# A decoder layer on one core: four rooms for value pages, three for key pages, transposes dealt out between matmuls, and an MLP in token halves

## The chip, the core and the metric

The kernel runs on one core of a Trainium2 chip. A core has a matrix engine (TensorE, PE in the rows; its weight loads are PEld), a vector engine (VectorE, DVE), an activation engine (ScalarE, ACT), a general engine (GpSimd, POOL) and SyncE (SP), which here only issues transfers. Each works through its own list of instructions in order; engines wait for each other on semaphores. Matmuls write to PSUM, eight banks of 128 partitions by 512 fp32 numbers. The metric is the device time of one execution in microseconds (us); lower is better.

## The reference, cut to what matters

One decoder layer is applied to 512 prompt tokens and to 64 sample tokens (8 sequences of 8 tokens, each with 512 cached positions in four pages of 128):

```python
h = rms_norm(x, ln1_pre) * (1 + sc1) + sh1            # shifts, scales, gates from c @ ada_w
u, q, k, v, qi, ki, wi = split(h @ w_in)
mixed = concat(pool_mix(u), sparse_attention(q, qi, wi, k, v, ki))   # top 128 or 130 keys a query
x = x + g1 * rms_norm(mixed @ w_out, ln1_post)
h = rms_norm(x, ln2_pre) * (1 + sc2) + sh2
f = square(relu(h @ w_ff1)) @ w_ff2                   # 1024 -> 4096 -> 1024
x = x + g2 * rms_norm(f, ln2_post)
```

The samples' keys and values come partly from the paged caches `cache_k` and `cache_v`, through `page_table`. All is fp32.

## The kernel before

Every large product is split for accuracy: an operand is stored as a high part (`fp32r`, rounded by ScalarE) and a low part (the rest, by VectorE), and hi·hi + hi·lo + lo·hi are summed in PSUM. A weight of 1 MB (a "piece": 1024 rows by 256 columns, or 512 by 512) comes by DMA into `raw`, is split into `w_split` by ScalarE (`hi_until`) and VectorE (`lo_until`), and is then used. Both buffers have two rooms.

The program is written out by hand, one list of instructions for each engine; their order is the order of the code. Its stages:

1. **Head.** The first eight `ada` pieces give shift and scale as rows (`modulation`), which are turned into columns in `mod_t` (`turned_modulation`). The normalised tokens are transposed in eight chunks of 128 features (`turned_hidden`); ScalarE scales and shifts each chunk into `stage`, rounds it into `act_hi`, VectorE makes `act_lo`. The first projection (`qi`) goes through the eight chunks in order (`first_pair`).
2. **Projections, indexer, top-k, prompt attention.** `lg` are the logits of one of 32 (query block, head) pairs, `pv` their values. In between, the other 16 `ada` pieces are used.
3. **Cached attention of the samples.** For each sequence b, SyncE loads four key pages and four value pages (256 KB each; `load_pages`), TensorE turns the keys (`turn_pages`, banks `KT`), then for each pair of sequences bp comes `sample_logits`, the softmax on VectorE and ScalarE, `turn_sample_probs`, `sample_values` and `turn_sample_output`. Keys have two rooms in `pages`, values two in `v_pages`; b uses room b % 2. Values are loaded from the last prompt `pv` on; a room's next keys after its last `KT` bank, its next values after `pvR` of the pair.
4. **Output projection** (`wo`), residual, second norm; `turned_hidden(1)` transposes the eight chunks and then the samples' rows.
5. **MLP**, in four quarters of `w1` (16 pieces in all) and `w2`. For a piece of `w1`, `project` makes two chunks of 128 hidden features for the 512 prompt tokens (moving operand `act_hi`, `act_lo`, 128x512), then the 64 samples by rows: the samples' hi and lo parts (`act_s`, 128 columns) are the weights and the piece's hi and lo the moving operand (`rows_s`, eight matmuls of 512 columns). The two halves of that result are added and turned by `fold_pending` (plain fp32, through `halves_mlp`). ScalarE takes relu, VectorE squares, and both split again into `hid_hi`, `hid_lo`, `hid_s` for `w2` (`by_token`).

All matmuls are issued in the helper `mm` (line 747), all transposes in `turn` (line 750), nearly all ScalarE work in `run` (line 1294), so names of tiles tell more than lines.

## Time and profile before

| | |
|---|---|
| Median of 3 runs | 910.16 us (906.89 to 914.69) |
| The profiled execution | 910.76 us, its span 909.1 us |
| TensorE busy | 832.8 us, 92% of the span |
| VectorE, ScalarE, GpSimd busy | 443.4, 329.2, 88.9 us |
| Mean granted TensorE clock | 0.957 of full speed |
| Bytes moved | 105.85 MB, 116 GB/s on average |

The span runs from the first to the last instruction; 1.7 us of the device time lie outside it. A matmul's shown length includes a drain that overlaps the next one, so rates are read from the starts. In rows, `128*128 128x512` is a weight of 128 by 128 and a moving operand of 512 columns. An fp32 matmul stands twice in the trace, an fp32r matmul once.

### The profile page before, as it was taken

The numbers are of one execution on the slowest core, as the hardware profiler recorded it, in microseconds if no ns is written. First come the engines' busy times: TensorE is split into PE (matmuls) and PEld (weight loads), VectorE is DVE, ScalarE is ACT, GpSimd is POOL, SyncE is SP. The second block draws the span as 40 slices with busy tenths as digits, with TensorE's granted clock in tenths as the row PEclk, the third lists the DMA queues.
The fourth block names the chain that finished last, engine by engine and source line by source line (L and its number), as shares of the span: only waits on it lengthen the run. The fifth ranks groups of instructions, "written<-read, shape, count | busy, mean of one in ns | idle before, by whom it ended". The sixth has DMA issues, their size and how long they took to land.

```text
span 909.1 us, 11559 instructions
## 1 busy us (share of the span) xinstructions
PE 832.8 (92%) x4338; PEld 638.3 (70%) x4338; DVE 443.4 (49%) x819; ACT 329.2 (36%) x611; POOL 88.9 (10%) x144
## 2 busy tenths in 40 slices
PE   2799999799988987789969999999999999999997
PEld 0377557587745566547847888888888888888875
DVE  0351666999767864412655422243333343244255
ACT  2462542133355653403463422343213241134332
POOL 2141301011623320010010000000000000000000
PEclk9989999798989998969979999999999999999999
DMA  9833311022367677682112123222212222321202
GB/s 318 293 101 104 102 47 45 16 91 92 96 226 267 212 250 252 218 313 67 47 47 93 49 91 93 70 69 93 90 54 89 93 72 67 93 93 50 90 0 105
DMA packets 68779, 105.85 MB, mean 116 GB/s; under 512 B 6986, under 2 KB 32214, under 8 KB 68714
## 3 DMA queue, kind: packets, MB, share of 16 engines
q1 hardware_dynamic: 64194, 96.48, 32.3%
q0 software_dynamic: 3296, 6.39, 2.3%
q10 hardware_dynamic: 1232, 2.23, 0.7%
q8 instruction: 35, 0.57, 0.3%
q14 instruction: 22, 0.18, 0.1%
HBM read 100.04 MB, written 5.15 MB: 116 GB/s over the span
## 4 chain that ended last, share of the span: by engine, by line
PE 80%; DVE 6%; DMA 6%; ACT 3%; issue 2%; SPq 2%; DVEq 0%; POOL 0%; ACTq 0%
PE bank L747 77%; PE bank L750 3%; DMA pages<-in_ada_w 2%; DMA pages<-in_cache_k 2%; SPq L562 2%; DVE score L1817 1%; DMA raw<-in_ada_w 1%; DVE small L1813 1%; ACT w_split L1269 1%; ACT stage L1294 1%; DMA v_pages<-in_cache_v 1%; DVE w_split L496 1%; DVE x_res L1998 0%; DMA out_v_p<-stage 0%; DVE x_nrm L1714 0%
## 5 line engine op out<-in xcount | busy, mean ns | idle before, releaser
L747 PE MATMUL bank<-act_hi,w_split 128*128 128x512 f32 (+1 forms) x800 | 265.5, 401 | 5.5 <-DVE q_lo L1698 5.5
L747 PEld LDWEIGHTS bank<-act_hi,w_split 128*128 128x128 f32 (+1 forms) x800 | 152.0, 190 | 42.6 <-issue 7.4
L496 DVE TENSOR_TENSOR w_split<-raw,w_split 128x2048 fp32r<-128x2048 f32 (+2 forms) x47 | 105.5, 2247 | 127.0 <-ACT w_split L1269 126.9
L747 PE MATMUL bank<-w_split,hid_hi 128*128 128x512 f32 x512 | 159.0, 392 | 0.0
L747 PE MATMUL bank<-act_lo,w_split 128*128 128x512 f32 (+1 forms) x400 | 157.9, 395 | 0.0
L1269 ACT ACTIVATE w_split<-raw 128x2048 fp32r<-128x2048 f32 (+2 forms) x48 | 89.3, 1862 | 96.1 <-PE bank L747 96.0
L747 PEld LDWEIGHTS bank<-w_split,hid_hi 128*128 128x128 f32 x512 | 95.9, 188 | 20.9
L747 PE MATMUL bank<-w_split,hid_lo 128*128 128x512 f32 x256 | 100.3, 392 | 0.0
L747 PEld LDWEIGHTS bank<-act_lo,w_split 128*128 128x128 f32 (+1 forms) x400 | 76.3, 191 | 15.1
L1294 ACT ACTIVATE stage<-bank 128x512 f32<-128x512 f32 (+3 forms) x51 | 30.0, 589 | 98.3 <-PE bank L747 91.3
L747 PE MATMUL bank<-w_split,act_s 128*128 128x512 f32 (+1 forms) x248 | 60.7, 387 | 1.5 <-DVE out_t L2004 1.5
L747 PE MATMUL bank<-w_split,act_hi 128*128 128x512 f32 x192 | 61.2, 400 | 0.0
L747 PEld LDWEIGHTS bank<-w_split,hid_lo 128*128 128x128 f32 x256 | 48.1, 188 | 10.4
L2048 DVE TENSOR_TENSOR stage<-stage 128x512 f32<-128x512 f32 x32 | 22.2, 692 | 67.3 <-ACT stage L1294 65.8
L747 PEld LDWEIGHTS bank<-w_split,act_s 128*128 128x128 f32 x248 | 46.0, 188 | 11.3 <-issue 1.9
L747 PEld LDWEIGHTS bank<-w_split,act_hi 128*128 128x128 f32 x192 | 36.6, 193 | 8.3 <-issue 0.8
L747 PE MATMUL bank<-w_split,act_lo 128*128 128x512 f32 x96 | 38.1, 397 | 0.0
L747 PE MATMUL bank<-w_split,hid_s 128*128 128x512 f32 x128 | 32.0, 392 | 2.2 <-DVE out_t L2076 2.2
L1294 ACT ACTIVATE probs<-probs,small 128x128 f32<-128x128 f32 (+4 forms) x36 | 20.9, 580 | 31.7 <-DVE small L1893 20.5
L747 PE MATMUL bank<-raw,c_pad 128*32 128x512 f32 x160 | 27.4, 764 | 5.3 <-DMA raw<-in_ada_w 5.2
L1294 ACT ACTIVATE stage_s<-bank 128x128 f32<-128x128 f32 (+1 forms) x24 | 9.2, 384 | 62.5 <-PE bank L747 62.5
L1294 ACT ACTIVATE half_s<-bank 64x512 f32<-64x512 f32 x10 | 5.9, 595 | 65.5 <-PE bank L747 65.5
(247 smaller groups left out, 1061.2 us busy)
## 6 DMA issues: line engine op xcount, KB each, us to landing
raw<-in_w_ff SPq DMA_DIRECT2D x32, 1024.0 KB, 5.4
raw<-in_ada_w SPq DMA_DIRECT2D x20, 1024.0 KB, 5.3
raw<-in_w_in SPq DMA_DIRECT2D x10, 1024.0 KB, 5.5
pages<-in_cache_k SPq DMA_DIRECT2D x32, 256.0 KB, 5.3
v_pages<-in_cache_v SPq DMA_DIRECT2D x32, 256.0 KB, 4.2
pages<-in_ada_w SPq DMA_DIRECT2D x4, 1024.0 KB, 12.5
raw<-in_w_out SPq DMA_DIRECT2D x4, 1024.0 KB, 6.9
x_in<-in_x_prompt SPq DMA_DIRECT2D x1, 2048.0 KB, 14.6
```

The source lines that it names most:

```text
L496: return ops.tensor_tensor(lo, r, hi.bitcast(F32), ALU.subtract)
L562: sp.dma_start(slots[:, b % 2, g, :], cache[bass.ds(page[b * NPG + g], 1)].rearrange("o p n -> (o p) n"))\
L747: return nc.tensor.matmul(out, lhsT, rhs, start=start, stop=stop, skip_group_check=True)
L750: return nc.tensor.transpose(out, in_, cc("ident")[0:k, 0:k])
L1269: return nc.scalar.activation(hi, r, ACT.Copy)
L1294: return nc.scalar.activation(out, in_, func, **kw)
L1813: link(nc.vector.max(top8[0:r, :], buf))
L1817: link(nc.vector.match_replace(buf, top8[0:r, :], buf, TAKEN))
L2048: nc.vector.tensor_tensor(stage[:, n % 2, :], stage[:, n % 2, :], stage[:, n % 2, :], ALU.mult)\
```

## The change

- **Cached attention.** `v_pages` gets four rooms and `k_more` is a third room for keys. Both lie where the prompt's `q_hi` to `k_lo` and `qiv_hi` were. The values of sequences 0 to 3 are loaded once the last two `lg` banks are full; the third key room after the last `pv`. The two first `wo` pieces are loaded after these values and after the keys of sequence 4, where they came before all of them.
- **Head.** `turned_modulation(0)` is cut into quarters between the `ada` pieces; four of the eight chunks and the samples' rows are transposed between the steps of the first `qi` matmuls. On ScalarE the split of the first `qi` piece stands ahead of the last `ada` rows, on VectorE ahead of `mod_t`.
- **MLP.** The tokens are two halves of 256 prompt and 32 sample tokens (HN = 288), in `tok_hi` and `tok_lo`. A unit is 128 hidden features for one half: 24 matmuls with 288 moving columns. A piece has four units, in three banks that rotate. `rows_s`, the fold and `halves_mlp` are gone from the MLP. The samples' rows are transposed first; three chunks follow, and the other five stand between the steps of the first three units.

```diff
@@ plan_banks @@
-            take(("w1", 8 * f + 2 * i), 0), take(("w1", 8 * f + 2 * i + 1), 1)
-            take(("w1R", 4 * f + i), 2), take(("w1S", 4 * f + i), 2)
+            for u in range(4):
+                take(("w1", 8 * f + 2 * i + u // 2, u % 2), (4 * i + u) % 3)
@@ SyncE @@
-            for n in range(AT[("ada", 12)] + 2, AT[("wo", 0)] + 2):
+            for n in range(AT[("ada", 12)] + 2, AT[("wo", 0)]):
                 load_piece(n)
+            full(sp, ("lg", N_AT - 2))
+            full(sp, ("lg", N_AT - 1))
+            for b in range(4):
+                load_pages(b, cv, v_rooms, v_page_in)
+            load_piece(AT[("wo", 0)])
             full(sp, ("pv", N_AT // 2 - 1))
...
+            load_pages(2, ck, k_rooms, k_page_in)
+            for b in (3, 4):
+                full(sp, ("KT", b - 3, 3))
+                load_pages(b, ck, k_rooms, k_page_in)
+            load_piece(AT[("wo", 1)])
+            for b in (5, 6):
+                full(sp, ("KT", b - 3, 3))
+                load_pages(b, ck, k_rooms, k_page_in)
+            full(sp, ("pvR", 0))
+            for b in (4, 5):
+                load_pages(b, cv, v_rooms, v_page_in)
...
@@ TensorE, head @@
+            for i in range(4):
                 modulation(i)
+            out = claim(("modT", 0))
+            turned_quarter(out, 0)
+            modulation(4)
+            turned_quarter(out, 1)
+            modulation(5)
...
+                    if kc < 4:
+                        turned_chunk(0, x_nrm, kc + 4)
+                    elif kc == 4:
+                        turned_rows(0, x_nrm)
@@ TensorE, MLP @@
+            def unit_step(out, hi, lo, j, x, kc):
+                cols = slice(128 * j, 128 * j + 128)
+                mm(out[:, 0:HN], hi[:, kc, cols], tok_hi[:, kc, x, :], kc == 0, False)
+                mm(out[:, 0:HN], hi[:, kc, cols], tok_lo[:, kc, x, :], False, False)
+                return mm(out[:, 0:HN], lo[:, kc, cols], tok_hi[:, kc, x, :], False, kc == KC - 1)
...
+                    for kc in range(KC):
+                        pe.wait_ge(S["h_hi"], KC + kc + 1)
+                        pe.wait_ge(S["h_low"], KC + kc + 1)
+                        for out, (j, x) in zip(outs, units):
+                            last = unit_step(out, hi, lo, j, x, kc)
...
+                        if kc + 3 < KC:
+                            turned_chunk(1, out_t, kc + 3)
@@ VectorE @@
+            lo_until(AT[("qi", 0)] + 1)
             turned_hidden(0)
-            lo_until(AT[("qi", 0)] + 1)
...
+                else:
+                    stage_rows(1)
                 if j:
                     normalise(2, LATE[j - 1], out_t, x_res)
```

SyncE's list between the last `ada` pieces and the first keys of the cached attention, before; a name in brackets is a semaphore that the row waits for (`bank_full7`: the last `pv`; `bank_full0` to `bank_full2`: a `KT` bank).

```order
L535 DMA raw<-in_w_out 128x4x512 [waits ada_half]
L535 DMA raw<-in_w_out 128x4x512 [waits bank_full0]
L562 DMA v_pages<-in_cache_v 128x512 [waits bank_full7]
L562 DMA v_pages<-in_cache_v 128x512 x7
L562 ISA [waits bank_full0]
L562 DMA pages<-in_cache_k 128x512
```

The same place after; `bank_full4,bank_full3` are the last two `lg`.

```order
L576 DMA v_pages<-in_cache_v 128x512 [waits bank_full4,bank_full3]
L576 DMA v_pages<-in_cache_v 128x512 x7
...
L548 DMA raw<-in_w_out 128x4x512 [waits ada_half]
L576 DMA k_more<-in_cache_k 128x512 [waits bank_full7]
L576 DMA k_more<-in_cache_k 128x512 x3
L576 DMA pages<-in_cache_k 128x512 [waits bank_full0]
L576 DMA pages<-in_cache_k 128x512 x3
L576 ISA [waits bank_full1]
L576 DMA pages<-in_cache_k 128x512
```

The value pages now stand ahead of the first `wo` piece and wait for logits instead of values; keys of sequence 2 wait for the last `pv` alone.

TensorE in the MLP before, at the end of a piece of `w1`, the start of the next one, and its fold.

```order
L747 MATMUL bank1<-act_lo,w_split 128x512
L747 MATMUL bank1<-act_hi,w_split 128x512
L747 MATMUL bank2<-w_split,act_s 128x512 [waits bank_free2]
L747 MATMUL bank2<-w_split,act_s 128x512 x7
L747 MATMUL bank0<-act_hi,w_split 128x512 [waits bank_free0,lo_ready]
L747 MATMUL bank0<-act_lo,w_split 128x512
...
L747 MATMUL bank0<-act_hi,w_split 128x512
L747 MATMUL bank2<-cst,halves_mlp 128x64 [waits bank_free2]
L747 MATMUL bank2<-cst,halves_mlp 128x64 x3
L747 MATMUL bank1<-act_hi,w_split 128x512 [waits bank_free1]
```

The same place after, from the end of one unit into the next.

```order
L770 MATMUL bank2<-tok_lo,w_split 128x288
L770 MATMUL bank2<-tok_hi,w_split 128x288
L770 MATMUL bank0<-tok_hi,w_split 128x288 [waits bank_free0]
L770 MATMUL bank0<-tok_lo,w_split 128x288
L770 MATMUL bank0<-tok_hi,w_split 128x288 x2
L770 MATMUL bank0<-tok_lo,w_split 128x288
```

The sample rows and the folds are gone, and every matmul is 288 columns wide.

TensorE in the head before (`c_pad` rows are `ada` pieces, `mod_rows` the turn of the modulation, `x_nrm` chunks of tokens).

```order
L747 MATMUL bank<-raw,c_pad 32x512 x8
L750 MATMUL bank<-cst,rows_in 128x52
L750 MATMUL bank<-cst,x_nrm 128x128 x16
L747 MATMUL bank<-pages,c_pad 32x512 x8
L747 MATMUL bank<-cst,mod_rows 128x9 x16
L750 MATMUL bank<-cst,x_nrm 128x128 x16
L750 MATMUL bank<-cst,x_nrm 128x64 x8
L747 MATMUL bank<-act_hi,w_split 128x512
L747 MATMUL bank<-act_lo,w_split 128x512
```

The same place after.

```order
L770 MATMUL bank<-cst,mod_rows 128x9 x4
L770 MATMUL bank<-raw,c_pad 32x512 x4
L770 MATMUL bank<-cst,mod_rows 128x9 x4
L770 MATMUL bank<-raw,c_pad 32x512 x4
L773 MATMUL bank<-cst,rows_in 128x52
L770 MATMUL bank<-pages,c_pad 32x512 x4
L770 MATMUL bank<-cst,mod_rows 128x9 x4
L770 MATMUL bank<-pages,c_pad 32x512 x4
L773 MATMUL bank<-cst,x_nrm 128x128 x8
L770 MATMUL bank<-cst,mod_rows 128x9 x4
L773 MATMUL bank<-cst,x_nrm 128x128 x8
L770 MATMUL bank<-act_hi,w_split 128x512
```

Three of the four quarters of the modulation's turn now stand between `ada` pieces, and the matmuls with `act_hi` begin after four chunks instead of eight and the samples' rows.

## Rows read from the trace of the kernel before

**Rows 1.** The page, part 4: shares by engine of the chain that ended last.
```profile
PE 80%; DVE 6%; DMA 6%; ACT 3%; issue 2%; SPq 2%; DVEq 0%; POOL 0%; ACTq 0%
```

**Rows 2.** Busy time by stretch: us, PE, PEld, DVE, ACT, POOL, PEclk, DMA, GB/s.
```profile
473.00:600.00 127.00, 127.00 (x564) 102.60 (x563) 46.69 (x50) 43.95 (x59) 0.00 (x0) 1.00 0.24 75
```

**Rows 3.** Instructions in order of time, TensorE, MLP: start, us, operation, count.
```profile
501.23 1.98 PE L747 MATMUL bank<-w_split,act_s 128*128 128x512 f32 x8
...
508.48 1.00 PE L747 MATMUL bank<-cst,halves_mlp 128*128 128x64 f32 x8
...
522.09 1.00 PE L747 MATMUL bank<-cst,halves_mlp 128*128 128x64 f32 x8
```

**Rows 4.** The same view, two earlier stretches with narrower moving operands.
```profile
90.24 1.15 PE L747 MATMUL bank<-w_split,act_s 128*128 128x272 f32 x8
...
329.11 0.28 PE L747 MATMUL bank<-keys,qiv_hi 128*128 128x256 f32 x1
...
329.58 0.28 PE L747 MATMUL bank<-turned_hi,qiv_lo 128*128 128x256 f32 x1
```

**Rows 5.** One tile (act_s, MLP): weight loads' durations min/median/max ns.
```profile
L747 PEld LDWEIGHTS bank<-w_split,act_s x128: 187/188/188, 483.3 to 847.5; 128*128 128x128 f32 x128
```

**Rows 6.** Order of time, TensorE, cached attention; brackets: idle before, releaser.
```profile
321.79 0.40 PE L747 MATMUL bank<-k_hi,q_lo 64*128 64x512 f32 x2
...
345.12 6.08 PE L750 MATMUL bank<-cst,pages 128*128 128x128 f32 x32 [4.03 <-DMA pages<-in_cache_k]
351.04 0.60 PE L750 MATMUL bank<-cst,probs 128*128 128x128 f32 x4
...
357.42 3.94 PE L750 MATMUL bank<-cst,pages 128*128 128x128 f32 x32
...
373.41 3.25 PE L750 MATMUL bank<-cst,pages 128*128 128x128 f32 x16 [2.19 <-DMA pages<-in_cache_k]
...
390.47 1.94 PE L747 MATMUL bank<-v_pages,p_t 128*32 128x128 f32 x32 [2.01 <-DMA v_pages<-in_cache_v]
...
397.29 2.96 PE L747 MATMUL bank<-mod_rows,cst 128*128 128x512 f32 x3
```

**Rows 7.** The same view of SyncE's DMA issues.
```profile
333.47 3.68 SPq L562 DMA_DIRECT2D v_pages<-in_cache_v  x8
```

**Rows 8.** The same view of VectorE, cached attention.
```profile
354.84 0.56 DVE L1937 CUSTOM_DVE_ANT_0 probs<-bank,small 128x384 f32<-128x384 f32 x1 [2.91 <-PE bank L747]
...
357.69 0.23 DVE L1952 TENSOR_TENSOR p_new<-probs,cst 128x64 f32<-128x64 f32 x1
...
379.55 4.49 DVE L496 TENSOR_TENSOR w_split<-raw,w_split 128x2048 fp32r<-128x2048 f32 x2 [1.41 <-ACT w_split L1269]
```

**Rows 9.** The same view of ScalarE there.
```profile
377.61 3.72 ACT L1269 ACTIVATE w_split<-raw 128x2048 fp32r<-128x2048 f32 x2
```

**Rows 10.** The same view of all engines, before the first projection.
```profile
38.74 1.90 ACT L1269 ACTIVATE w_split<-raw 128x2048 fp32r<-128x2048 f32 x1
...
43.36 2.29 DVE L496 TENSOR_TENSOR w_split<-raw,w_split 128x2048 fp32r<-128x2048 f32 x1
43.36 0.78 ACT L1294 ACTIVATE stage<-bank,mod_t 128x512 f32<-128x512 f32 x1 [2.72 <-DVE mod_t L1729]
...
50.60 0.79 PE L747 MATMUL bank<-act_hi,w_split 128*128 128x512 f32 x1
```

**Rows 11.** The same view, into the MLP.
```profile
462.88 0.17 DVE L1709 RECIPROCAL rstd<-rstd 128x1 f32<-128x1 f32 x1 [0.68 <-ACT rstd L1294]
...
472.46 0.50 PE L747 MATMUL bank<-act_hi,w_split 128*128 128x512 f32 x1
```

**Rows 12.** Busy time by stretch, columns as in rows 2.
```profile
36.00:42.80 6.80, 5.92 (x51) 4.15 (x49) 0.13 (x1) 2.40 (x2) 1.68 (x3) 1.00 0.71 223
42.80:53.00 10.20, 7.80 (x30) 5.70 (x31) 6.68 (x9) 9.20 (x14) 4.54 (x9) 0.50 0.41 83
...
341.10:345.10 4.00, 0.00 (x0) 0.00 (x0) 1.12 (x6) 0.00 (x0) 0.00 (x0) 0.76 1.05 393
```

More of the change, by code:

```diff
@@ L51 @@
 UW = 16 + TP + DB * SEG
+HP, HS = TP // 2, TS // 2
+HN = HP + HS
 def t5_bucket(n):
@@ L285, in build_program @@
         w_split = sb("w_split", [128, NSPLIT, 4096], F32R)
-        act_hi = sb("act_hi", [128, KC, TP], F32R)
-        act_lo = sb("act_lo", [128, KC, TP], F32R)
+        first = ExitStack()
+        act_hi = sb("act_hi", [128, KC, TP], F32R, first)
+        q_s = sb("q_s", [128, 4, TS], stack=first)
+        k_s = sb("k_s", [128, 4, TS], stack=first)
+        act_lo = sb("act_lo", [128, KC, TP], F32R, first)
+        ki_s = sb("ki_s", [128, TS], stack=first)
+        wi_t = sb("wi_t", [8, TS], stack=first)
+        ident_r = sb("ident_r", [128, 128], F32R, first)
+        first.close()
+        tok_hi = sb("tok_hi", [128, KC, 2, HN], F32R)
+        tok_lo = sb("tok_lo", [128, KC, 2, HN], F32R)
         act_s = sb("act_s", [128, KC, 2 * TS], F32R)
@@ L402, in build_program @@
         stage_out = [sem("stage_out0"), sem("stage_out1")]
-        k_page_in = [sem("k_page_in0"), sem("k_page_in1")]
-        v_page_in = [sem("v_page_in0"), sem("v_page_in1")]
+        k_page_in = [sem(f"k_page_in{i}") for i in range(3)]
+        v_page_in = [sem(f"v_page_in{i}") for i in range(4)]
+        k_rooms = [pages[:, 0, :, :], pages[:, 1, :, :], k_more[:, :, :]]
+        v_rooms = [v_pages[:, i, :, :] for i in range(4)]
         block = ctx.enter_context(nc.Block())
@@ L585, in _ @@
+            full(sp, ("pvR", 0))
+            for b in (4, 5):
+                load_pages(b, cv, v_rooms, v_page_in)
+            full(sp, ("KT", 4, 3))
+            load_pages(7, ck, k_rooms, k_page_in)
+            full(sp, ("pvR", 1))
+            for b in (6, 7):
+                load_pages(b, cv, v_rooms, v_page_in)
             for n in range(AT[("wo", 0)] + 2, len(PIECES)):
@@ L801, in _, with turned_quarter, turned_rows @@
-            for i in range(6):
-                modulation(i)
+            def turned_quarter(out, g):
+                evacuated(pe, ("ada", 2 * g + 1))
+                for j in range(4 * g, 4 * g + 4):
+                    last = mm(out[:, 9 * j:9 * j + 9], mod_rows[:, 128 * j:128 * j + 128], cc("sel_t"), True, True)
+                return last
+            def turned_rows(k, src):
+                out = claim(("hTS", k))
+                for kc in range(KC):
+                    last = turn(out[:, TS * kc:TS * kc + TS], src[0:TS, NT, 128 * kc:128 * kc + 128], TS)
+                done(last, ("hTS", k))
@@ L803, in _, with turned_chunk @@
+            def turned_chunk(k, src, kc):
+                out = claim(("hT", k, kc))
+                for t in range(NT):
+                    last = turn(out[:, 128 * t:128 * t + 128], src[:, t, 128 * kc:128 * kc + 128], 128)
+                done(last, ("hT", k, kc))
+            for i in range(4):
+                modulation(i)
+            out = claim(("modT", 0))
[3 more added lines that the diff above has]
+            modulation(5)
             pe.wait_ge(S["small_in"], 96)
@@ L804, in _ @@
             done(turn(claim("rowsT")[:, 0:52], rows_in[:, :], 52), "rowsT")
-            turned_hidden(0, x_nrm, range(4), False)
-            for i in range(6, 8):
-                modulation(i)
-            turned_modulation(0)
-            turned_hidden(0, x_nrm, range(4, KC))
+            modulation(6)
+            turned_quarter(out, 2)
+            modulation(7)
+            pe.wait_ge(S["normed"], NT + 1)
+            for kc in range(2):
+                turned_chunk(0, x_nrm, kc)
+            done(turned_quarter(out, 3), ("modT", 0))
@@ L811, in _ @@
+            for kc in range(2, 4):
+                turned_chunk(0, x_nrm, kc)
             hidden_ready = []
@@ L1160, in turn_pages @@
                     for g in range(NPG):
-                        last = turn(out[:, 128 * g:128 * g + 128], pages[:, b % 2, g, 128 * c:128 * c + 128], 128)
+                        last = turn(out[:, 128 * g:128 * g + 128], k_rooms[b % 3][:, g, 128 * c:128 * c + 128], 128)
                     done(last, ("KT", b, c))
@@ L1328, in turned_hidden @@
                 act.wait_ge(S["mod_ok"], 2 * (k + 1))
+                if k:
+                    act.wait_ge(S["hs_staged"], 2)
+                    run(tok_hi[:, :, :, HP:HN], stage_s[:, :, :].rearrange("p c (x t) -> p c x t", x=2)).then_inc(S["hs_hi"], 1)
                 for kc in range(KC):
```

179 lines of the change are left out of this document (93 added, 86 removed).

## The prediction

> **What bounds the kernel now.** I read the chain that ended last first: four fifths of it are TensorE [rows 1], so a wait elsewhere counts only where TensorE stands still for it. Then busy time by stretch. In the MLP TensorE has no gap at all: 127.0 of 127.0 us, at a granted clock of 1.00 [rows 2]. There only fewer matmul columns help. The gaps are in three other places, and the instructions in order of time show what ends them: the cached attention waits for pages [rows 6], the head for the first projection's operands [rows 10], the MLP for its first chunk [rows 11]. The change touches these four places, so the sum has four terms. It is made against the profiled execution, 910.8 us (span 909.1 and 1.7 outside it), which lies 0.6 above the median of 910.16.
>
> **The MLP's units.** Before, a piece takes from one fold to the next 522.09 - 508.48 = 13.61 us [rows 3]. It holds 48 chunk matmuls and 8 sample matmuls of 512 columns, and the fold. Between the start of the sample matmuls at 501.23 and the fold at 508.48 lie 32 matmuls of 512 columns [rows 3]: 7.25 / 32 = 0.2266 us each. After, a piece is 4 units x 24 = 96 matmuls of 288 columns. No row has 288, but two are near. Five matmuls of 256 columns start within 0.47 us, 0.1175 each; eight of 272 take 1.15 us, less the 0.28 that one lasts, so 0.124 each [rows 4]. The line through 256 and 512 rises by 0.000426 us a column and gives 0.1175 + 32 x 0.000426 = 0.131 for 288. A piece is then 96 x 0.131 = 12.6 us, 1.02 less, and 16 pieces save **16.3 us**. Bounds: if 288 cost as much a column as 256 do, 0.1322, the saving is 14.7; if as little as 512 do, 0.1275, it is 21.9. I take the line, since the 272 row lies within 0.001 of it. Of the 1.02, the fold gives 0.92 (13.61 - 56 x 0.2266) and 1,024 columns fewer give 0.44; 40 more matmuls, each with a fixed 0.0084 on that line, take 0.34 back.
>
> The Trainium skill, "TensorE: Matmul & The Clock Gate", section "Back-to-back issue gap", puts a warm matmul at its columns over 2.4 GHz and 2.5 ns. That is 122.5 ns for 288 columns, an estimate by which a piece takes 11.8 us and the whole comes to about 866. The rows disagree: for 512 columns the rule says 216 ns and they show 227, so the measurement decides.
>
> Nothing else in a piece should reach TensorE. A unit lasts 3.1 us and a bank comes back two units (6.3 us) later. ScalarE needs two relus and two roundings for a pair of units, VectorE a square and two subtractions, and both are busy for about a third of this stretch [rows 2]. The weight split at a piece's end delays a relu by about 2 us, less than the 6.3. If that cover failed, each piece would lose the excess, up to 2 us.
>
> **Into the MLP.** Before, the last norm's reciprocal is at 462.88 after an idle wait of 0.68, and the first matmul at 472.46, since all transposes come first [rows 11]. After, VectorE puts two sample operations ahead of that reciprocal, about 0.75 each, of which the idle time takes 0.7: norm 0.8 later, first transpose about 464.8. A chunk needs four transposes (32 take 3.94 us at full clock [rows 6], so 0.5, or 1.0 at half), scaling (0.78, as in the head [rows 10]), rounding and subtraction (about as long): first matmul at about 468.2, 4.3 earlier. But five chunks, 5 x 0.5 = 2.5 us, now stand between matmuls, where they were hidden by the wait. Net 1.8; but the granted clock can fall to half around such a start, as in the head (0.50 from 42.8 to 53.0 [rows 12]), and then falls on matmuls instead of transposes, at up to 3 us. So between -1 and +2; I take **1.0 saved**.
>
> **Head.** Before, VectorE splits the first weights (2.29 us) after `mod_t`, ahead of the first `act_lo`, and TensorE begins the projection only at 50.60, after all transposes [rows 10]. After, ScalarE's split (1.90 us) waits for the weights, which land at about 38: the DMA queues are busy for 0.71 of 36.0 to 42.8 [rows 12], so until about 40.8, and one more megabyte behind them takes near 3 us. Then come the last modulation rows, a quarter of the turn (the full one has 32 records) and `mod_t`, with VectorE's split just ahead of it at about 42. The first scaling stays near 43, where it was (43.36), but the low part no longer queues behind 2.29 us, and TensorE can start at about 45, 5.6 earlier. It pays for four chunks and the sample rows between matmuls, 2.6 us at full clock, 5 at half, and at the clock of 0.50 [rows 12] much of this may run at half. Between 0 and 4; I take **1.5 saved**.
>
> **Cached attention.** TensorE waits 4.03 us for keys of sequence 2, 2.19 for a later pair, 2.01 for values [rows 6], 8.2 us in these three alone, and the work behind each is slow: 32 transposes take 6.08 us after the first wait and 3.94 us without one [rows 6]. After, values wait for the last `lg`, whose matmuls end at 322.2, instead of 333.47 [rows 6, 7]: 11 us sooner. From there I follow TensorE. Logits of pair 0 end at 341.1, where the 4.03 begins. Two sequences of keys take 4.0; probabilities, logits and values of one pair take 357.42 - 351.04 = 6.4 [rows 6]; VectorE's softmax takes from 354.84 to 357.92, 3.1 [rows 8], hidden after the first pair. So keys 2 and 3 end at 345.3, the first softmax lets go at about the same time, pair 0 ends at 352.0, keys 4 and 5 at 356.0, pair 1 at 362.8 with its output, keys 6 and 7 at 367, pair 2's output with the logits of pair 3 near 371.
>
> Here the next limit stands: ScalarE's split of the two `wo` pieces (3.72 us) and VectorE's (4.49, it waits for them) come right after pair 1's output, ahead of the last softmax [rows 8, 9]. They start near 368.3 instead of 377.6, VectorE's ends near 375, softmax at 378, then transposes, values and output of the last pair, 5.5 to 7.5 us with their handovers and a possible half clock. The gates come at 383.5 to 386 instead of 397.29 [rows 6]. Saved 11.3 to 13.8, I take **12.5**. Bounds: 6, if key pages 2 still come as late as before (below), and 15, if the `wo` splits don't bind.
>
> Edits with one answer: the first key rooms and the `ada` loads don't move; GpSimd's list is unchanged; the output projection and the second MLP product keep their matmuls.
>
> **Sum.** 16.3 + 1.0 + 1.5 + 12.5 = 31.3; 910.8 - 31.3 = **879.5 us**.
>
> **Rivals.**
> 1. *The pages stay late.* SyncE's list now holds 16 value pages and a `wo` piece, 5.2 MB, ahead of the third key room. With the four key pages that is 6.3 MB from 322.6 on. At the 393 GB/s of 341.1 to 345.1 [rows 12] the keys land near 339; under 286 GB/s they land at 345, where they came before. For it speaks that one queue carries all; against it that the queue stands still before 333 for want of a room. It costs the 4.03 and about 2 of slow work behind it: 885.5.
> 2. *Slower: the weight load sets the pace.* Each matmul loads its own weights, and a load lasts 188 ns [rows 5]. 512 columns cover that at 227; 288 columns at 131 don't, if a load can't begin before the one ahead has finished. Then a piece takes 96 x 0.188 = 18.0 us, 4.4 more than before, 16 pieces 71 more, and with the other terms 910.8 - 15.0 + 71 = 967. It decides from 0.142 us a matmul (13.61 / 96) for the MLP by itself, and from 0.152 ((16 x 13.61 + 15) / 1536) for the whole. Against it: the 272-column rows have the same loads and come every 0.124 us. The same page of the Trainium skill, section "Step-by-step: what each phase is for", lets a load run under the matmul before it; these rows agree.
> 3. *The small matmuls cost no more a column than the large ones.* Then the units save 21.9, not 16.3: 874.
> 4. *Both new starts give nothing*, because the half clock falls on matmuls and the transposes between them cost what the earlier start gives: 882.
>
> **How the numbers follow.** Chances: forecast, 874.5 to 884, 0.62; rival 1, 0.14; rival 3, 0.10; rival 4 falls into the forecast's range; rival 2, 0.04; several misses on the gain's side with a result still under 901, 0.06; a new stall that leaves less than 9 us, 0.04. The range of 868 to 891 takes in rivals 1, 3 and 4 and one further term at its lower bound (879.5 + 6.5 + 2.5 = 888.5, and 3 for scatter among runs); below it and above it I leave about 0.15. A measurement here tells about 1% from no change, which is 901 to 919. Faster by more: 0.93; within: 0.03; slower: 0.04.
>
> **What would show it.** Units every 3.1 to 3.2 us in the MLP with TensorE still full and `tok_hi` matmuls 0.131 apart; VectorE and ScalarE never the releaser of a unit's bank. In the cached attention no idle time that a page ends; value pages issued right after the last `lg`; the gates near 385 less what the head gives; the last wait there ended by VectorE's softmax behind the `wo` split. First matmuls 5 to 6 us earlier in the head and 4 in the MLP, each followed by transposes between matmuls. The prediction is wrong if the distance of unit matmuls is above 0.135, if the third key room lands after TensorE asks for it, or if one of the starts moves later.

## The result

The changed kernel takes 887.38 us (median of 4 executions, 884.9 to 889.27) where the kernel before took 912.42 beside it: a ratio of 0.9728, 95% interval 0.9667 to 0.979. In a second series, described below, it was 0.9714 (0.9677 to 0.9751). The forecast was 879.5 with a range of 868 to 891, so it held the sign and the range; the gain is about 25 us, where 31.3 were forecast.

The page of the changed kernel, parts 1, 4 and 5 (in the last: busy us, mean ns, and idle time before with what ended it):

```profile
PE 815.1 (92%) x4850; PEld 657.7 (74%) x4850; DVE 441.2 (50%) x819; ACT 325.5 (37%) x627; POOL 89.0 (10%) x144
...
PE 81%; DVE 7%; DMA 5%; ACT 3%; issue 2%; SPq 1%; DVEq 0%; POOL 0%; ACTq 0%
...
L770 PE MATMUL bank<-tok_hi,w_split 128*128 128x288 f32 x1024 | 207.8, 297 | 0.6 <-DVE tok_lo L1774 0.6
```

TensorE has 512 matmuls more than before and is busy for 17.7 us less. The chain is bounded as before [rows 1]. The units' matmuls waited 0.6 us in all, once, for the first chunk.

Busy time by stretch (us; PE, PEld, DVE, ACT, POOL; granted clock; DMA share; GB/s): the stretch of rows 2, then the second quarter's `w1` and its `w2`:

```profile
473.00:600.00 127.00, 127.00 (x775) 114.64 (x774) 45.65 (x52) 42.26 (x68) 0.00 (x0) 1.00 0.26 83
566.48:617.36 50.88, 50.88 (x385) 50.88 (x384) 20.98 (x26) 19.06 (x34) 0.00 (x0) 1.00 0.25 83
617.36:668.65 51.29, 51.29 (x227) 42.07 (x225) 17.47 (x17) 9.23 (x8) 0.00 (x0) 1.00 0.26 82
```

TensorE is still full at full clock [rows 2]. Four pieces are 384 matmuls in 50.88 us, so 0.1325 us each and 12.72 us a piece, where it was 13.61 [rows 3].

TensorE in order of time, cached attention (start, us; in brackets the idle time before and what ended it):

```profile
343.31 2.00 PE L773 MATMUL bank<-cst,k_more 128*128 128x128 f32 x16 [1.71 <-DMA k_more<-in_cache_k]
345.95 2.00 PE L773 MATMUL bank<-cst,pages 128*128 128x128 f32 x16 [0.64 <-DMA pages<-in_cache_k]
...
374.79 1.08 PE L770 MATMUL bank<-v_pages,p_t 128*32 128x128 f32 x32 [0.66 <-ACT p_t L1369]
...
378.98 0.44 PE L773 MATMUL bank<-cst,pv_rows 128*128 128x128 f32 x2 [1.40 <-ACT pv_rows L1369]
...
386.47 4.08 PE L770 MATMUL bank<-mod_rows,cst 128*128 128x512 f32 x8
```

The three long waits for pages [rows 6] are down to 1.71 and 0.64, both at the start; the gates begin at 386.47, where it was 397.29. What SyncE, ScalarE and VectorE do there, in the same view:

```profile
322.86 9.11 SPq L576 DMA_DIRECT2D v_pages<-in_cache_v  x16
...
333.98 1.95 SPq L576 DMA_DIRECT2D k_more<-in_cache_k  x4
```

```profile
370.10 3.72 ACT L1344 ACTIVATE w_split<-raw 128x2048 fp32r<-128x2048 f32 x2
```

```profile
372.04 4.49 DVE L509 TENSOR_TENSOR w_split<-raw,w_split 128x2048 fp32r<-128x2048 f32 x2 [1.41 <-ACT w_split L1344]
```

Values are issued 10.6 us earlier than before [rows 7]; the splits of the `wo` pieces stand where they stood [rows 8, 9], 7.5 us earlier.

The head of the changed kernel, all engines, same view:

```profile
40.30 2.29 DVE L509 TENSOR_TENSOR w_split<-raw,w_split 128x2048 fp32r<-128x2048 f32 x1 [9.17 <-ACT w_split L1344]
...
43.20 0.78 ACT L1369 ACTIVATE stage<-bank,mod_t 128x512 f32<-128x512 f32 x1 [2.44 <-DVE mod_t L1808]
...
45.57 0.47 PE L770 MATMUL bank<-act_hi,w_split 128*128 128x512 f32 x1 [2.78 <-DVE act_lo L1774]
...
59.16 2.29 DVE L509 TENSOR_TENSOR w_split<-raw,w_split 128x2048 fp32r<-128x2048 f32 x1 [1.04 <-ACT w_split L1344]
...
62.20 0.47 PE L770 MATMUL bank<-act_hi,w_split 128*128 128x512 f32 x1 [0.92 <-DVE qiv_lo L1774]
```

The first matmul is at 45.57 instead of 50.60 [rows 10], after a split that VectorE now does ahead of `mod_t`. At 62.20 TensorE waits again: VectorE's split of the second `qi` piece stands behind the samples' rows and ahead of `qiv_lo`. TensorE, into the MLP:

```profile
451.88 2.82 PE L773 MATMUL bank<-cst,out_t 128*128 128x128 f32 x12 [7.92 <-DVE out_t L1793]
455.34 0.58 PE L770 MATMUL bank<-tok_hi,w_split 128*128 128x288 f32 x1 [0.64 <-DVE tok_lo L1774]
...
455.96 0.68 PE L770 MATMUL bank<-tok_hi,w_split 128*128 128x288 f32 x2
...
456.44 0.44 PE L770 MATMUL bank<-tok_lo,w_split 128*128 128x288 f32 x1
```

The first matmul of the MLP is at 455.34 instead of 472.46 [rows 11]. But the two starting at 455.96 and the next at 456.44 are 0.24 apart, nearly twice the distance of the later ones. Busy time by stretch shows why: the granted clock is 0.50 there, until 460.4.

```profile
446.70:460.40 13.70, 7.88 (x34) 7.49 (x35) 7.85 (x12) 7.49 (x12) 0.87 (x1) 0.50 0.24 77
```

**Where the time went, by stages.** From the starts in order of time of each kernel, experiments included, I took six lengths. "Head" is the start of the eight 272-column matmuls [rows 4]; "prompt" goes from the first to the last group of `lg` matmuls; "cached" from the last `pv` matmul to the first of `wo`; "into MLP" from the last `act_hi` matmul of `wo` (0.23 us before its last one) to the first of `w2`, four pieces included; then the second quarter's `w1` and `w2`. All in us.

| profile of | head | prompt | cached | into MLP | w1 | w2 |
|---|---|---|---|---|---|---|
| before | 90.24 | 64.97 | 70.01 | 74.87 | 53.52 | 52.39 |
| changed | 87.98 | 67.77 | 56.83 | 72.49 | 50.88 | 51.29 |
| changed, second profile | 89.28 | 64.18 | 60.51 | 72.33 | 50.88 | 51.29 |
| cached part alone | 94.28 | 64.10 | 61.02 | 76.48 | 53.52 | 52.39 |
| head alone | 89.64 | 64.51 | 70.12 | 74.87 | 53.54 | 52.39 |
| MLP alone | 91.19 | 68.12 | 66.50 | 72.63 | 50.88 | 51.29 |
| late values | 90.89 | 67.54 | 64.15 | 72.43 | 50.88 | 51.29 |
| spread `wo` splits | 90.87 | 64.10 | 57.27 | 72.44 | 50.88 | 51.29 |
| early key room | 91.09 | 64.20 | 56.93 | 72.58 | 50.88 | 51.29 |
| both of these | 89.87 | 65.07 | 53.51 | 72.24 | 50.88 | 51.29 |
| turns first | 89.88 | 65.10 | 59.41 | 72.01 | 50.88 | 51.29 |
| 256 columns | 90.02 | 67.29 | 55.39 | 67.11 | 45.81 | 51.28 |
| quarter fold | 92.11 | 70.51 | 66.32 | 72.87 | 51.53 | 51.72 |

The second quarter of the MLP repeats to 0.02 us wherever the code is the same. The other stages do not: the prompt attention, whose code no kernel here changes, takes 64.1 to 70.5 us.

Nor does the last `w2`, which none of the six lengths holds. TensorE, after the same wait there, in the first and then in the second profile of the changed kernel:

```profile
849.71 3.54 PE L770 MATMUL bank<-w_split,hid_s 128*128 128x512 f32 x8 [2.21 <-DVE out_t L2168]
```

```profile
851.82 2.07 PE L770 MATMUL bank<-w_split,hid_s 128*128 128x512 f32 x8 [2.21 <-DVE out_t L2168]
```

In the first the granted clock is 0.50 from 849.5 to 852.9, in the second it stays at 1.00. From the first matmul of the last `w2` to the end the two take 61.45 and 59.95 us. The clock falls in this place in six of the thirteen profiles: the first of the changed kernel, cached part alone, head alone, MLP alone, early key room and turns first.

### The profile page after: what moved, and what is told of

The parts are those of the page before. It is cut to its first block, busy times and chain, and to the rows that moved or that the text cites. A ratio compares the mean times of both kernels' runs of the same rounds, so it can differ in the third digit from the quotient of the medians.

```text
span 883.1 us, 12590 instructions
## 1 busy us (share of the span) xinstructions
PE 815.1 (92%) x4850; PEld 657.7 (74%) x4850; DVE 441.2 (50%) x819; ACT 325.5 (37%) x627; POOL 89.0 (10%) x144
## 4 chain that ended last, share of the span: by engine, by line
PE 81%; DVE 7%; DMA 5%; ACT 3%; issue 2%; SPq 1%; DVEq 0%; POOL 0%; ACTq 0%
PE bank L770 78%; PE bank L773 3%; DMA pages<-in_ada_w 2%; ACT w_split L1344 1%; DVE score L1908 1%; DVE small L1904 1%; DMA pages<-in_cache_k 1%; DMA raw<-in_w_in 1%; DVE w_split L509 1%; DMA raw<-in_ada_w 1%; ACT stage L1369 1%; DMA out_v_p<-stage 1%; DVE x_res L2089 0%; DVE keys L1774 0%; DVE probs L1984 0%
## 5 line engine op out<-in xcount | busy, mean ns | idle before, releaser
L770 PE MATMUL bank<-tok_hi,w_split 128*128 128x288 f32 x1024 | 207.8, 297 | 0.6 <-DVE tok_lo L1774 0.6
L770 PEld LDWEIGHTS bank<-tok_hi,w_split 128*128 128x128 f32 x1024 | 165.9, 189 | 2.2 <-issue 2.0
L770 PE MATMUL bank<-tok_lo,w_split 128*128 128x288 f32 x512 | 151.6, 296 | 0.0
L770 PE MATMUL bank<-act_hi,w_split 128*128 128x512 f32 (+1 forms) x288 | 102.4, 416 | 9.2 <-DVE q_lo L1777 5.5
L770 PEld LDWEIGHTS bank<-tok_lo,w_split 128*128 128x128 f32 x512 | 96.9, 189 | 0.1
L1369 ACT ACTIVATE stage<-bank 128x288 f32<-128x288 f32 (+3 forms) x83 | 36.9, 447 | 121.6 <-PE bank L770 114.5
L770 PEld LDWEIGHTS bank<-act_hi,w_split 128*128 128x128 f32 (+1 forms) x288 | 55.2, 192 | 26.0 <-issue 9.6
L2143 DVE TENSOR_TENSOR stage<-stage 128x576 f32<-128x576 f32 x32 | 24.3, 759 | 76.0 <-ACT stage L1369 76.0
L770 PE MATMUL bank<-act_lo,w_split 128*128 128x512 f32 (+1 forms) x144 | 57.8, 401 | 0.0
L770 PEld LDWEIGHTS bank<-act_lo,w_split 128*128 128x128 f32 (+1 forms) x144 | 27.9, 194 | 5.2
```

Source lines behind the costliest of these rows:

```text
L770: return nc.tensor.matmul(out, lhsT, rhs, start=start, stop=stop, skip_group_check=True)
L1369: return nc.scalar.activation(out, in_, func, **kw)
L2143: nc.vector.tensor_tensor(st, st, st, ALU.mult).then_inc(S["w1_squared"], 1)
```

## The experiments

**One part at a time.** Three kernels, each the kernel before with one part of the change.

Cached part alone, its core:

```diff
-                        load_pages(b, cv, v_pages, v_page_in)
...
+            full(sp, ("lg", N_AT - 2))
+            full(sp, ("lg", N_AT - 1))
+            for b in range(4):
+                load_pages(b, cv, v_rooms, v_page_in)
...
+            load_pages(2, ck, k_rooms, k_page_in)
```

> The kernel before with only the part on the pages changed: four rooms for value pages and a third for key pages, loaded as in the changed kernel; head and MLP as before. Theory A (the ledger by stages: the gains are those of three parts that do not touch each other): 13.2 us less than the kernel before, nearly all of it between the last prompt matmul and the first out projection, so about 899 us where the kernel before takes 912.4; the first gate matmul some 10 to 11 us earlier than in the kernel before, the head and every MLP piece as before. Theory B (pages are ready earlier only because the head starts the prompt attention 2.3 us earlier, or the MLP's later work gives part of it back): less than 10 us.

Measured: 905.82 us beside 913.2 (ratio 0.9923, 0.9896 to 0.9951), 7.4 less. So neither theory as put: below 10, but for another reason than B names, since this kernel's head was no earlier. Its first wait is the one of the changed kernel, and longer; TensorE, same view:

```profile
348.17 3.27 PE L771 MATMUL bank<-cst,k_more 128*128 128x128 f32 x16 [2.60 <-DMA k_more<-in_cache_k]
...
392.97 5.76 PE L768 MATMUL bank<-mod_rows,cst 128*128 128x512 f32 x8
```

Transposes that take 2.00 us in the changed kernel take 3.27 here, and gates that take 4.08 take 5.76.

Head alone, its core:

```diff
-            turned_hidden(0, x_nrm, range(4), False)
...
+            turned_quarter(out, 0)
+            modulation(4)
...
+                    if k == 0 and kc < 4:
+                        turned_chunk(0, x_nrm, kc + 4)
```

> The kernel before with only the head changed: turns between the modulation's matmuls, and the splits of the first query piece ahead of the last modulation. Theory A (ledger): 2.3 us less until the first matmul of the prompt's scores, and the prompt attention as long as before (64.97 us from its first to its last score matmul), so 910 us where the kernel before takes 912.4. Theory B (the 2.8 us that the prompt attention lost in the changed kernel follow from the shift of the head, which moves where the clock falls): prompt attention 67 to 68 us here too, and the whole within 0.7 us of the kernel before.

Measured: 909.5 us beside 913.2 (0.9954, 0.9933 to 0.9974), 3.7 less, with a prompt attention of 64.51. Theory B falls: the head's shift does not lengthen the prompt attention.

MLP alone, its core:

```diff
-                    project("w1", 4 * f + i)
+                    hidden_units(4 * f + i)
```

> The kernel before with only the MLP changed: units of 256 prompt and 32 sample columns, no fold, and its own turns between matmuls. Theory A (ledger): 13.5 us from the pieces and 0.3 us at the start the other way, so 13.2 us less, about 899 us; a piece of 96 matmuls lasts 12.7 us where it lasted 13.6. Theory B (the pieces are only quicker because the cached attention hands over earlier and loads of weights run further ahead): a piece of 13.2 us or more, and under 8 us less in all.

Measured: 899.78 us beside 913.2 (0.9855, 0.9807 to 0.9902), 13.4 less, pieces as in the changed kernel. Theory A holds. The three parts give 7.4 + 3.7 + 13.4 = 24.5, the whole about 25 to 26: the parts add up.

**The same kernel again.** No edit.

> The changed kernel itself once more, for the spread of its stages between two profiled executions of the same code. Theory A (the stages' differences in one pair of profiles carry chance of where the clock falls): its prompt attention, first to last score matmul, lies anywhere between 64 and 68 us (67.78 in its first profile), its head up to 3 us later than in its first profile (87.98 us at the end of the key index projection), its stretch from the last prompt matmul to the first out projection 55 to 61 us, and its MLP quarters, where the clock does not fall, are the same to 0.1 us. Theory B (the stages are set by the code): every stage within 0.3 us of the first profile. The median by both some 887 us.

Measured: 886.9 us beside 913.08 (0.9714, 0.9677 to 0.9751). Theory A holds at every stage. Busy time by stretch of its prompt attention, after that of the first profile:

```profile
254.53:322.30 67.77, 59.48 (x388) 35.23 (x388) 50.68 (x179) 39.41 (x120) 23.14 (x37) 0.85 0.71 235
```

```profile
256.68:320.86 64.18, 56.80 (x389) 33.27 (x388) 50.36 (x177) 39.36 (x120) 23.18 (x37) 0.89 0.74 249
```

The same instructions, with VectorE and ScalarE busy for as long to 0.4 us; the granted clock is 0.85 in one and 0.89 in the other. And its gates, with the stretch around them:

```profile
386.97 5.83 PE L770 MATMUL bank<-mod_rows,cst 128*128 128x512 f32 x8
```

```profile
380.30:390.50 10.20, 9.14 (x87) 4.27 (x86) 0.45 (x2) 1.41 (x5) 1.88 (x3) 0.50 0.15 53
```

The clock is 0.50 until 390.5, into the gates, which then take 5.83 us. In the first profile it was back at full before they began, and they took 4.08. So in these two profiles a stage with waits has a length that is good only to 2 to 4 us.

**The splits off the last wait.** The changed kernel with the `wo` splits in earlier gaps:

```diff
@@ ScalarE, after p_t of pair bp @@
+                if bp < 2:
+                    hi_until(AT[("wo", 0)] + 1 + bp)
...
-                if bp == 1:
-                    hi_until(AT[("wo", 0)] + 2)
@@ VectorE, before the peaks of pair bp + 1 @@
+                if bp in (1, 2):
+                    lo_until(AT[("wo", 0)] + bp)
...
-                if bp == 1:
-                    lo_until(AT[("wo", 0)] + 2)
```

> The changed kernel with the splits of the two first out-projection pieces moved off the wait for the last softmax: ScalarE takes one high part in the gap before its second exponential of samples and one before its third, VectorE the low parts one pair later each, where both stood idle for 3 to 4 us. Theory A (the two splits in a row are what the cached attention waits for last): the waits of 0.66, 1.40, 0.28, 0.18 and 0.51 us between 374 and 382 us go, 3.0 us, and if the clock then does not fall the values and gates after them run in half their time, up to 3 us more: 3 to 6 us less than the changed kernel, 881 to 884.5 us beside 887.4. Theory B (the last softmax is a chain that nothing hides, whatever stands on ScalarE and VectorE): at most 1 us less.

Measured: 882.75 us (880.47 to 884.24; ratio to before 0.9648, 0.9604 to 0.9692), about 4.4 under the changed kernel's 886.9 to 887.4, as theory A has it. VectorE in order of time:

```profile
373.39 2.29 DVE L509 TENSOR_TENSOR w_split<-raw,w_split 128x2048 fp32r<-128x2048 f32 x1
...
376.81 0.56 DVE L2028 CUSTOM_DVE_ANT_0 probs<-bank,small 128x384 f32<-128x384 f32 x1 [1.13 <-PE bank L770]
```

The second low part is done 1.13 us before the last logits, so the softmax now waits for TensorE and for nothing else. The profile by itself shows less: the cached stage is 57.27 long, because this execution waited 3.17 us for `k_more`, with the transposes behind it at 3.53 us. From the transposes of keys 6 and 7 to the gates it takes 19.28 us, where the changed kernel's two profiles take 21.05 and 21.91, so the trace accounts for 2 to 3 of the 4.4. The intervals of the two ratios overlap a little (0.9677 is the lower end for the changed kernel); the pair of runs under "Both" settles it.

**The value pages late.** The changed kernel, rooms as they are:

```diff
-            full(sp, ("lg", N_AT - 2))
-            full(sp, ("lg", N_AT - 1))
-            for b in range(4):
-                load_pages(b, cv, v_rooms, v_page_in)
...
             load_pages(2, ck, k_rooms, k_page_in)
+            for b in (0, 1):
+                load_pages(b, cv, v_rooms, v_page_in)
```

> The changed kernel with its rooms as they are, but no value page is asked for before the prompt's last matmul: the first two value pages follow the third key page, the next two the fifth. Theory A (the early start of the 4 MB of value pages, 9.1 us of queue time, is what the cached attention gained): the stretch from the last prompt matmul to the first out projection, 56.8 to 61.0 us with the early loads and 66.5 to 70.1 without the change, is over 62 us, and the whole 3 to 8 us longer than the changed kernel's 887.4. Theory B (more rooms alone suffice, since the transfers then run back to back behind the transposes): within 1 us of it.

Measured: 894.32 us (891.09 to 896.18; 0.9781, 0.9753 to 0.9809), 7 more than the changed kernel. Theory A holds: with this order, the early start is worth about as much as the whole cached part. TensorE:

```profile
345.43 2.00 PE L773 MATMUL bank<-cst,k_more 128*128 128x128 f32 x16
...
352.99 3.67 PE L773 MATMUL bank<-cst,pages 128*128 128x128 f32 x16 [5.56 <-DMA pages<-in_cache_k]
```

SyncE, whose value pages now stand ahead of these key pages:

```profile
340.03 4.19 SPq L576 DMA_DIRECT2D v_pages<-in_cache_v  x8
344.41 5.32 SPq L576 DMA_DIRECT2D pages<-in_cache_k  x8
```

So the 7 us are those of late values together with the keys of sequence 3 behind them. The third key room is asked for after the last `pv` here as well, yet TensorE does not wait for it. Its four issues, in the changed kernel and then here (KB each, median us from issue to landing):

```profile
k_more<-in_cache_k SPq DMA_DIRECT2D x4, 256.0 KB, 6.5
```

```profile
k_more<-in_cache_k SPq DMA_DIRECT2D x4, 256.0 KB, 3.1
```

In the changed kernel they stand behind 16 value pages and a `wo` piece. Busy time by stretch, from the first value page's issue to the landing of `k_more`, has the DMA engines full (1.03):

```profile
322.90:343.30 20.40, 15.83 (x136) 10.97 (x134) 12.17 (x33) 8.65 (x22) 4.58 (x19) 1.00 1.03 372
```

**The third key page early.** The changed kernel with `k_more` and the fourth value room in exchanged places:

```diff
-            for b in range(4):
+            load_pages(2, ck, k_rooms, k_page_in)
+            for b in range(3):
                 load_pages(b, cv, v_rooms, v_page_in)
...
             full(sp, ("pv", N_AT // 2 - 1))
-            load_pages(2, ck, k_rooms, k_page_in)
             for b in (3, 4):
                 full(sp, ("KT", b - 3, 3))
                 load_pages(b, ck, k_rooms, k_page_in)
+            load_pages(3, cv, v_rooms, v_page_in)
```

> The changed kernel with the third key page in the place of the first value room, which comes free with the prompt's last scores, and loaded there at once; the fourth value page is loaded after the last prompt matmul instead. Theory A (the cached attention first waits for the third key page, whose room is free only at the last prompt matmul: 1.71, 2.60 and 3.17 us in three profiles, with the clock falling behind the wait in two): that wait and what follows it go, 2 to 4 us, 883.5 to 885.5 us beside 887.4. Theory B (the fourth key page, whose room is free only after the first transposes, is late by as much and takes the wait over): within 1 us of the changed kernel.

Measured: 884.99 us (882.99 to 886.52; 0.9677, 0.9659 to 0.9695). That lies where A put it, but its range overlaps the changed kernel's, so the median alone does not decide. In the trace the first wait for `k_more` is gone, while TensorE waits 0.81 us for the page behind it and 0.60 for the second use of `k_more`, so a part of the wait is handed over, as B has it.

**Both.** The spread splits and the early key page together.

> The third key page loaded early, as in the run before this one of the list, together with the splits of the two out-projection pieces spread over the idle gaps (measured alone at 882.75 us). Theory A (two separate limits, one at the start and one at the end of the cached attention): 2 to 4 us less than the spread splits alone, 878.7 to 880.8 us, and the stretch from the last prompt matmul to the first out projection 52 to 54 us. Theory B (one limit takes over from the other): 882 to 884 us.

Measured: 880.32 us (879.14 to 881.18; ratio to before 0.9636, 0.962 to 0.9652), cached stage 53.51 us. That is where theory A put it. Against the early key room alone, in the same series, the spread splits gain 4.7 us, and the two ranges lie apart. Against the spread splits alone the early key room gains 2.4, as it does in the run above, but the intervals overlap both times, so by time alone this second gain is not shown; the trace shows its wait gone. SyncE, then TensorE, in order of time:

```profile
322.26 1.93 SPq L576 DMA_DIRECT2D k_more<-in_cache_k  x4
```

```profile
340.82 2.00 PE L774 MATMUL bank<-cst,k_more 128*128 128x128 f32 x16
343.15 2.01 PE L774 MATMUL bank<-cst,pages 128*128 128x128 f32 x16 [0.33 <-DMA pages<-in_cache_k]
...
377.37 1.94 PE L771 MATMUL bank<-v_pages,p_t 128*32 128x128 f32 x32 [0.36 <-ACT p_t L1370]
...
382.45 4.09 PE L771 MATMUL bank<-mod_rows,cst 128*128 128x512 f32 x8
```

No first wait for `k_more`; what is left is 0.33 us for the page behind it and 0.61 when the room is used again, for sequence 5. This version beats both kernels.

**Fewer columns.** The changed kernel with `0:HP` (256) for `0:HN` in the three matmuls of `unit_step`:

```diff
-                mm(out[:, 0:HN], hi[:, kc, cols], tok_hi[:, kc, x, :], kc == 0, False)
+                mm(out[:, 0:HP], hi[:, kc, cols], tok_hi[:, kc, x, 0:HP], kc == 0, False)
```

> The changed kernel with units of 256 columns: the 32 columns of samples in each unit are left out of the MLP's first product, so the samples' rows of the result are those of other numbers. Theory A (a matmul costs by its columns): from the 256-column and 512-column rows of the kernel before, about 0.12 us each, so a piece of 96 lasts 11.5 us where it lasts 12.7, 1.2 us x 16 = 19 us less in all. Theory B (the load of the 128 x 128 weights ahead of each matmul sets the pace): 0.1325 us each as with 288 columns, and no change.

Measured once: 862.95 us. Busy time by stretch of its second `w1` quarter:

```profile
561.31:607.12 45.81, 45.81 (x385) 45.80 (x384) 20.97 (x26) 19.10 (x34) 0.00 (x0) 1.00 0.29 93
```

384 matmuls take 45.81 us, 0.1193 each. Theory A holds, theory B falls: with the same loads a matmul of 256 columns is 0.0132 quicker than one of 288. Four quarters save 4 x 5.07 = 20.3 us; the rest of the 24.4 to the changed kernel's median lies in the stages that vary, in a single run. In the changed kernel's units a load lasts 188 ns in the median, longer than the 119 to 133 from one matmul to the next, so loads overlap the matmuls before them.

**All turns first.** The changed kernel with eight chunks ahead of the units instead of three:

```diff
-            for kc in range(3):
+            for kc in range(KC):
                 turned_chunk(1, out_t, kc)
...
-                        if kc + 3 < KC:
-                            turned_chunk(1, out_t, kc + 3)
```

> The changed kernel with all eight chunks of the MLP's input transposed before its first units, none between them. Theory A (the turns between the units only move: what the earlier first matmul gains is given back by turns of 0.43 us and by units that run while the clock is still low): from the last out-projection matmul to the first matmul of the first down projection 72 to 73.5 us, where the changed kernel has 72.5 and the kernel before, with its longer pieces, 74.9; the whole within 1 us of the changed kernel. Theory B (as predicted: the first matmul 4.3 us earlier for 2.5 us of turns): 74 us or more, and 1.5 to 2 us slower.

Measured: 887.18 us (886.05 to 890.12; 0.9726, 0.9681 to 0.9771), "into MLP" 72.01. Theory A holds. TensorE:

```profile
461.14 0.65 PE L773 MATMUL bank<-cst,out_t 128*128 128x128 f32 x4 [0.67 <-ACT stage L1367]
461.55 0.38 PE L770 MATMUL bank<-tok_hi,w_split 128*128 128x288 f32 x1
...
461.89 0.42 PE L770 MATMUL bank<-tok_hi,w_split 128*128 128x288 f32 x2
```

The first matmul comes 16.9 us after the last of `wo`, where the changed kernel has 12.64 and the kernel before 17.08, but the clock is already full (it was 0.50 from 448.9 to 459.1), and nothing stands between the units.

**A quarter of the fold.** The kernel before with one of four small matmuls in each MLP fold:

```diff
+                        if kind == "w1":
+                            if j:
+                                last = mm(y, src[:, 128:256], cc("fold"), True, True)
+                            continue
```

> The kernel before with one of the four small matmuls of each fold in the MLP, so that the samples' part of its result is that of other numbers. Theory A (56 matmuls of 512 columns at 0.2266 us are worth what 96 of 288 columns at 0.1325 are, 12.69 and 12.72 us, so the fold is all that the units save): three quarters of 0.92 us a piece go, 0.69 us x 16 = 11 us less than the kernel before, about 902 us. Theory B (the gain is in the eight matmuls of the samples' rows, and the fold lies in time that is idle anyway): under 3 us less.

Measured: 903.06 us beside 913.08 (0.9889, 0.9837 to 0.9941), 10.0 less. TensorE in order of time:

```profile
511.08 0.33 PE L747 MATMUL bank<-cst,halves_mlp 128*128 128x64 f32 x2
...
524.02 0.33 PE L747 MATMUL bank<-cst,halves_mlp 128*128 128x64 f32 x2
```

A piece takes 12.94 us instead of 13.61 [rows 3]: 0.67 less for three quarters of the fold, so 0.89 for all of it. Theory A holds: TensorE pays the whole fold, and the units save hardly more than that, 0.935 a piece.

## Why the prediction came out as it did

Right in sign and within its range, too large by 6 us. The stages that vary are compared here by means over all profiles that have the same code there; the ranges of a stage are 3 to 6 us wide, so its mean gain is good to some 2 us.

**Units: 16.3 forecast, 15.0 found.** A quarter saves 2.64 in `w1` and 1.10 in `w2`, 3.74, four quarters 15.0; of the 1.10 some 0.89 is the last piece's fold, which had stood behind the first `w2` matmuls (the quarter fold saves 0.67 there). For the other 0.2 no run shows the cause. The step that failed in size is the cadence: 0.131 from the line through 256 and 512 columns, 0.1325 found, just above the bound of 0.1322. The line was right and its lower point was wrong. The 0.1175 for 256 columns came from five starts within 0.47 us [rows 4]. All 87 full-clock steps between such matmuls in the same trace average 0.1188, and the 384 matmuls of the 256-column run give 0.1193. The line through 0.1193 and 0.2266 rises by 0.000419 a column and gives 0.1193 + 32 x 0.000419 = 0.1327. So 96 matmuls of 288 columns (12.72) cost what 56 of 512 did (12.69), and the fold is nearly the whole gain: 16 pieces at 0.89 are 14.2 of the 15.0. Rival 2, the load's pace, falls with the 256-column run. Rival 3 falls too: it needed 0.1275. The Trainium skill, "TensorE: Matmul & The Clock Gate", section "Back-to-back issue gap", gives columns over 2.4 GHz and 2.5 ns for an isolated warm matmul, which the prediction did not say. By it 288 columns would take 122.5 ns, an estimate; in this row of loads and matmuls 132.5 were measured, so the 866 stays out of reach.

**Into the MLP: 1.0 saved forecast, about nothing found.** The start came 4.4 us earlier (17.08 - 12.64), as forecast (4.3). In the first pair of profiles "into MLP" is 2.38 shorter, but its pieces alone, with three folds inside, should have made it 2.64 shorter, so 0.3 is lost. By means (three profiles of the old code with whole folds, 75.41; seven of the new, 72.45) 0.3 is saved. In the first pair 4.4 + 0.3 = 4.7 were paid where 2.5 were taken: the turns stand 1.62 us apart at full clock, 0.43 more than the nine matmuls between them (9 x 0.1325), so five are 2.2, and from 455.34 to 460.4 the units ran at half clock, which is about 5.06 / 2 = 2.5 more. The half clock on matmuls was named as a bound and sized at up to 3; the value taken, 1.0 of a net 1.8, left 0.8 for it. Rival 4 was right here. The old order does not guarantee a full clock either: in the cached part alone, with all turns first, it was 0.50 again from 468.1 to 471.5, on the first matmuls, and "into MLP" took 76.48.

**Head: 1.5 forecast, 2.0 found.** Nine profiles with the new head have its end at 89.95 on average (87.98 to 91.09), four with the old one at 91.96 (90.24 to 94.28). The first matmul came 5.0 earlier (5.6 forecast) in the first pair of profiles. Alone it measured 3.7 (2.4 to 6.1).

**Cached attention: 12.5 forecast, 9.6 found.** Five profiles with the new code and none of the further moves (changed, its second, cached part alone, turns first, 256 columns) average 58.63, four with the old code 68.24. The pair of the first two profiles alone would have said 13.2, and the part measured by itself 7.4 (4.5 to 9.5). The early value pages work as put: where they are loaded late, 7 us are gone. Two steps of the forecast stood against each other. The last limit, the `wo` splits, was named rightly, and spreading them gave 4.4 and 4.7. The first, "keys 2 and 3 end at 345.3" without a wait, failed: the third key room's page landed after TensorE asked for it, by 1.71 us in the first profile and 2.60 in the cached part alone, with transposes at 3.27 for 2.00 behind it there. This was named as a sign of a wrong prediction. Its room comes free only with the last `pv`, 11 us after the value rooms; in the place of a value room there is no first wait. The late room alone does not make the page late, since with late values the same room is filled without a wait. It is the transfers ahead of it, as rival 1 put it: the sum there has 6.3 MB at 393 GB/s, done near 339, while 372 GB/s over 20.4 us were 7.6 MB, done at 343.3. Rival 1 was right in that the keys are late, wrong in size: the wait is 1.57 to 3.17 us in six profiles, not 4.03. What remains open is how far the low clock of a stage follows from its waits and how far from chance: the gates took 4.08 or 5.83 us in two profiles of one code.

**Prompt attention: unchanged forecast.** The first pair of profiles showed 2.8 us more, the second profile 0.8 less than before. That is the clock (0.85 against 0.89; before, 0.89), not the change; why it differs between executions stays open.

**Sum.** 15.0 + 0.3 + 2.0 + 9.6 = 26.9, measured 25.0 and 26.2. Of the 4.4 by which the forecast's 31.3 lies above this sum, 2.9 are the cached attention, 1.3 the units and 0.7 the MLP's start, with 0.5 the other way in the head. Only the head's miss went the other way, so the range holds the result with little help from misses that cancel; inside the units the cadence alone cost 2.1, of which 0.8 came back in `w2`.

## What to carry to other kernels

Before a fixed cost per instruction is read off a line, its points must come from long rows: five starts were 1.5% off, and 87 in the same trace would have given 0.132 for 288 columns where 0.1325 was found. When transfers are moved ahead, give the rooms that come free first, and the first places in the queue, to what is asked for first: here the third key page had to wait for the last room and then for the value pages ahead of it, which were issued from 322.86 on and first used at 351.47. An earlier start after a long idle time may run at half clock (0.50 until 460.4 here, after an idle time of 7.92 us and twelve transposes), so a start gained by dealing out transposes between matmuls can be worth nothing.

## What the runs showed that I had not expected

The granted clock makes stages with waits uneven between executions of one code: the prompt attention took 64.18 and 67.77 us in two profiles of the changed kernel, the cached attention 60.51 and 56.83, in opposite directions, and the spans were 883.1 and 883.8. The last `w2` lost 1.5 us in the first of them alone, in a product that TensorE else runs at full clock. Comparing one profile with one other by stages had credited the cached attention with 13.2 us and charged the prompt attention with 2.8; neither held over more profiles.
